# Transposes of the probabilities one step further behind the scores, in two of three attention stages of a fused layer kernel

## What is computed

```python
# mixing: heads A (8, window 128, with sinks), heads B (8: compressed, selected and windowed branches, gated and added)
x = x + 0.5 * swiglu(rms_norm(x, ffn1_norm), ffn1_w_in, ffn1_w_out)
o_a = banded_attention(q_a, k_a, v_a, tbl[:, :8], 128, sinks_a)
o_b = gates[0] * o_cmp + gates[1] * o_sel + gates[2] * o_win
x = x + concatenate([o_a, o_b]) @ w_mix_out
x = x + 0.5 * swiglu(rms_norm(x, ffn2_norm), ffn2_w_in, ffn2_w_out)
# second block, layer 0: chunked attention with a bias by distance; layer 1: attention over latent keys and values
s = q @ k.T * scale + bias
p = softmax(where(valid, s, NEG_INF))
h = h + g1 * ((p @ v) @ wo)
h = h + g2 * conv_ffn(...)
```

## Time and profile before

| | |
|---|---|
| median of 3 runs | 2225.38 us (2224.84 to 2227.58) |
| span of the profiled execution | 2227.7 us |
| TensorE matmul / weight load busy | 98% / 82% |
| VectorE, ScalarE, GpSimd busy | 57%, 40%, 12% |
| mean granted TensorE clock | 0.996 of full |
| mixing with the start of its output matmul | about 483 to 622 us of the span |
| chunked with the start of its output matmul | about 1150 to 1230 us of the span |

### The profile page before, as it was taken

The page is one execution under the profiler, slowest core; times in us unless marked ns, Lnnn a source line. Parts: engine busy times, 40 slices in busy tenths (PEclk is TensorE's granted clock), DMA queues, the critical chain, the costliest instruction groups (busy, mean ns, idle before and its releaser), DMA issues.

```text
span 2227.7 us, 30871 instructions
## 1 busy us (share of the span) xinstructions
PE 2183.2 (98%) x11681; PEld 1820.5 (82%) x11681; DVE 1276.1 (57%) x2136; ACT 899.4 (40%) x1492; POOL 267.9 (12%) x445
## 2 busy tenths in 40 slices
PE   8999999998999999999999999999999999999998
PEld 6888888877888888888888888888878888888887
DVE  5764763557843363365347766465476766545654
ACT  4222223456742222225237544234364755332343
POOL 2110220035400020010017000000000430000000
PEclk9999999999999999999999999999999999999999
DMA  8964993231033274264331333332313212323332
GB/s 265 287 202 131 312 303 104 94 88 39 30 114 106 76 256 149 83 228 159 95 96 49 90 101 88 104 94 85 114 50 97 65 48 76 100 89 104 94 92 97
DMA packets 260212, 270.42 MB, mean 121 GB/s; under 512 B 9190, under 2 KB 202365, under 8 KB 260109
## 3 DMA queue, kind: packets, MB, share of 16 engines
q1 hardware_dynamic: 238381, 190.40, 28.8%
q0 software_dynamic: 21728, 78.63, 10.3%
HBM read 265.72 MB, written 12.72 MB: 125 GB/s over the span
## 4 chain that ended last, share of the span: by engine, by line
PE 84%; DVE 6%; ACT 5%; DMA 3%; issue 2%; POOL 1%; SPq 0%; DVEq 0%; POOLq 0%; ACTq 0%
PE bank L345 15%; PE bank L346 15%; PE bank L347 15%; PE bank L351 11%; PE bank L353 11%; PE bank L352 11%; PE bank L1855 2%; PE bank L1830 2%; PE bank L1808 2%; DMA raw<-in_ffn_w_in_dram 1%; DVE w_lo L328 1%; POOL probs L2026 1%; ACT w_hi L324 1%; ACT probs L1902 1%; ACT xT_hi L773 1%
## 5 line engine op out<-in xcount | busy, mean ns | idle before, releaser
L345 PE MATMUL bank<-xT_hi,w_hi 128*128 128x512 f32 (+1 forms) x1624 | 620.7, 382 | 7.2 <-DVE w_lo L328 3.8
L346 PE MATMUL bank<-xT_lo,w_hi 128*128 128x512 f32 (+1 forms) x1624 | 618.3, 381 | 0.0
L347 PE MATMUL bank<-xT_hi,w_lo 128*128 128x512 f32 (+1 forms) x1624 | 618.3, 381 | 0.0
L328 DVE TENSOR_TENSOR w_lo<-raw,w_hi 128x2048 fp32r<-128x2048 f32 (+2 forms) x200 | 410.9, 2055 | 319.7 <-ACT w_hi L324 317.9
L324 ACT ACTIVATE w_hi<-raw 128x2048 fp32r<-128x2048 f32 (+3 forms) x201 | 345.9, 1721 | 456.2 <-PE bank L353 398.2
L345 PEld LDWEIGHTS bank<-xT_hi,w_hi 128*128 128x128 f32 x1624 | 304.5, 188 | 69.8 <-DVE w_lo L328 4.2
L347 PEld LDWEIGHTS bank<-xT_hi,w_lo 128*128 128x128 f32 x1624 | 304.6, 188 | 59.4
L346 PEld LDWEIGHTS bank<-xT_lo,w_hi 128*128 128x128 f32 x1624 | 304.6, 188 | 58.1
L351 PE MATMUL bank<-w_hi,hid_hi 128*128 128x512 f32 x704 | 274.1, 389 | 0.0
L353 PE MATMUL bank<-w_hi,hid_lo 128*128 128x512 f32 x704 | 273.9, 389 | 0.0
L352 PE MATMUL bank<-w_lo,hid_hi 128*128 128x512 f32 x704 | 273.9, 389 | 0.0
(11 more groups left out here) (330 smaller groups left out, 2766.8 us busy)
## 6 DMA issues: line engine op xcount, KB each, us to landing
raw<-in_ffn_w_in_dram SPq DMA_DIRECT2D x40, 1024.0 KB, 6.1
raw<-in_f_win_dram SPq DMA_DIRECT2D x40, 1024.0 KB, 6.0
mod_w<-in_mod_w_dram POOLq DMA_DIRECT2D x48, 512.0 KB, 5.5
mod_w_more<-in_mod_w_dram POOLq DMA_DIRECT2D x48, 512.0 KB, 5.9
raw<-in_ffn_w_out_dram SPq DMA_DIRECT2D x24, 768.0 KB, 4.6
raw<-in_f_wout_dram SPq DMA_DIRECT2D x24, 768.0 KB, 4.4
raw<-in_a_wqkv_dram SPq DMA_DIRECT2D x12, 1024.0 KB, 5.2
skewed_strips<-bias_strips POOLq DMA_DIRECT2D x32, 320.0 KB, 7.0
```

Of the source, the lines that this page charges most:

```text
L328: dve.tensor_tensor(out=w_lo[:, slot, :n], in0=raw[:, slot, :n], in1=w_hi[:, slot, :n].bitcast(f32), op=ALU.subtract).then_inc(lo_done, 1)
L345: pe.matmul(o, lhsT=w[0], rhs=xs[0], start=first, stop=False)
L346: pe.matmul(o, lhsT=w[0], rhs=xs[1], start=False, stop=False)
L347: return pe.matmul(o, lhsT=w[1], rhs=xs[0], start=False, stop=last)
```

## The change

`PairAttention` gets a `lag` and a rule for the places in `probs`. With lag 1, which latent attention keeps, the order is as before. With lag 2, for mixing and chunked, TensorE does in iteration k scores of k, values of k-3 and transposes of k-2; copies are those of k-2, and the split of bank 7 moves back by one iteration too. There are three places for probabilities and for inverse sums, which move from `stat` to `small`. Mixing has a rule of its own for the places, so that its early steps stay clear of `cmp_w1`. One iteration more is needed to drain, and a third piece of the output matmul is laid into it, so that one piece instead of two stands behind the last values.

```diff
-        probs_0 = take("probs_0", [P, 6, SEQ], at=xT_at)
+        probs_0 = take("probs_0", [P, 9, SEQ], at=xT_at)
...
-        probs_1 = take("probs_1", [P, 6, SEQ], at=xT_at)
+        probs_1 = take("probs_1", [P, 9, SEQ], at=xT_at)
...
             def inverses(self, k, i, m=1):
-                at = 8 + 4 * (k % 2) + i
-                return stat[:, at:at + m]
+                at = 24 + 4 * (k % (self.lag + 1)) + i
+                return small[:, at:at + m]
...
-                for k in range(len(self.steps) + 2):
+                lag = self.lag
+                for k in range(len(self.steps) + lag + 1):
                     if k in beside:
                         beside[k](pe)
                     if k < len(self.steps):
                         self.scores_pe(pe, k)
                     if k in behind:
                         behind[k](pe)
-                    if k >= 2:
-                        self.values_pe(pe, k - 2)
-                    if 1 <= k <= len(self.steps):
-                        self.transposes_pe(pe, k - 1)
+                    if k > lag:
+                        self.values_pe(pe, k - lag - 1)
+                    if lag <= k < len(self.steps) + lag:
+                        self.transposes_pe(pe, k - lag)
...
+                    out_of, copied = k - lag - 1, k - lag
...
-                    if 1 <= k <= len(self.steps):
-                        self.copies(act, k - 1, "act", (0,))
+                    if 0 <= copied < len(self.steps):
+                        self.copies(act, copied, "act", (0,))
...
-                        if k >= 2:
-                            dve.wait_ge(self.t, self.after("t", k - 2))
+                        if k > lag:
+                            dve.wait_ge(self.t, self.after("t", k - lag - 1))
...
+        def probs_0_at(k):
+
+            if k < BANDED - 1:
+                return ((0, 1), (3, 4), (2, 5))[k % 3]
+            return ((6, 7, 8), (3, 4, 5), (0, 1, 2))[(k - BANDED + 1) % 3]
...
-                              probs_0, q0_hi, q0_lo)
+                              probs_0, q0_hi, q0_lo, 2, probs_0_at)
...
-        att_chunked = PairAttention(chunked, probs_1, q1_hi, q1_lo)
+        att_chunked = PairAttention(chunked, probs_1, q1_hi, q1_lo, 2)
...
             def beside(self):
                 k = len(self.att.steps)
-                return {k: lambda pe: self.gemm.piece(pe, 0, 0, [0]), k + 1: lambda pe: self.gemm.piece(pe, 0, 0, [1])}
+                return {k + n: lambda pe, n=n: self.gemm.piece(pe, 0, 0, [n]) for n in range(self.att.lag + 1)}
 
             def pe(self, pe, norm):
-                self.gemm.piece(pe, 0, 0, [2, 3])
+                self.gemm.piece(pe, 0, 0, range(self.att.lag + 1, TOK))
                 self.gemm.piece(pe, 0, 1, range(TOK))
```

More of the change, by code:

```diff
@@ L1717, in program, with __init__ @@
         class PairAttention:
-            def __init__(self, groups, probs, hi, lo):
+            def __init__(self, groups, probs, hi, lo, lag=1, places=None):
                 self.groups, self.probs, self.hi, self.lo = groups, probs, hi, lo
+                self.lag = lag
+                self.places = places or (lambda k: range(3 * (k % (lag + 1)), 3 * (k % (lag + 1)) + 3))
                 self.steps = [step for group in groups for step in group["steps"]]
@@ L1757, in prob @@
             def prob(self, k, unit):
-                at = 3 * (k % 2) + unit.bank
-                return self.probs[:, at, unit.col:unit.col + unit.n]
+                return self.probs[:, self.places(k)[unit.bank], unit.col:unit.col + unit.n]
             def least(self, k, i, m=1):
@@ L1888, in out_act @@
             def out_act(self, act, k):
-                act.wait_ge(self.o, self.after("o", k - 2))
-                act.activation(self.hi[:, self.last[k - 2], :], bank[7][:, :], ACT.Copy).then_inc(self.h, 1)
+                act.wait_ge(self.o, self.after("o", k))
+                act.activation(self.hi[:, self.last[k], :], bank[7][:, :], ACT.Copy).then_inc(self.h, 1)
             def out_dve(self, dve, k):
-                g = self.last[k - 2]
+                g = self.last[k]
                 dve.wait_ge(self.h, self.g0 + g + 1)
@@ L1935, in dve @@
                         behind[k](dve)
-                    early = k - 2 in self.last and self.steps[k - 2].windows is not None
+                    early = out_of in self.last and self.steps[out_of].windows is not None
                     if early:
-                        self.out_dve(dve, k)
+                        self.out_dve(dve, out_of)
                     large = step and step.windows is None and step.sink is None
@@ L1942, in dve @@
                         dve.reciprocal(self.inverses(k, 0, 2), self.sums(k, 0, 2)).then_inc(self.r, 1)
[L1943 to L1946, removed]
+                    if 0 <= copied < len(self.steps):
+                        self.copies(dve, copied, "dve")
+                    if out_of in self.last and not early:
+                        self.out_dve(dve, out_of)
                     if large:
```

16 lines of the change are left out of this document (9 added, 7 removed).

## The result

The changed kernel takes 2231.42 us (median of 21 runs, 2228.31 to 2234.57), the kernel before, run beside it, 2226.69 (21 runs). The ratio is 1.0018, with a 95% interval from 1.0013 to 1.0024: slower by 2.9 to 5.3 us (the medians differ by 4.7), where I had forecast faster by 1.1. The profiled execution of after has a span of 2230.3 us.

What follows compares the result with a forecast made beforehand. No engine was taken as full; waits closing each stage's loop, notably scaled probabilities to transposes, bound it. Mixing -4.1, chunked +1.3 and clock +1.7 gave -1.1 us: 2225.38 to 2224.3 us, 8-in-10 range 2218.5 to 2230.5.

Steps and rivals of the forecast that it cites:

- Mixing, banded steps: Early mixing: small matmuls of step 4 end 6.4 us earlier, the bias of step 8 starts 8.2 us earlier.
- four steps give 1.9 us: Banded steps up to step 8: each costs VectorE some 4.1 us instead of 4.7 to 5.3.
- Mixed groups: Later mixing: groups of 18.79 us shorten by 0.3 to 0.5 each, to VectorE's limit of 18.25 to 18.5.
- Ends: End of mixing and of chunked: 2.5 us of backlog plus a new 2.2 us wait for the weights' split, each.
- nothing upstream lets the split start sooner: Stage end: ScalarE's L1890 of the last group precedes the weights' split and waits for last values; wait of 2.2 us.
- Chunked: Chunked stage: last scores 3.4 us earlier, then 2.5 of backlog and 2.2 of wait, together +1.3 us.
- every other order keeps its distance: Both stages: the change cuts only the link from scaled probabilities to transposes; no size given.
- the period falls to 7.35: Chunked: a group takes 7.35 us instead of 7.64 (bounds 7.25 and 7.64), from three engines' loads.
- Clock: Behind the two new waits of 2.2 us: one fall to half clock of two, +1.7 us (bounds 0 and 3.4).
- The rule of the Trainium skill: GpSimd and VectorE: by their shared SBUF interfaces, more overlap would lengthen GpSimd's rows, 2.7 to 3.1 us in chunked.
- rival 3: Later groups: chunked stays at 7.64 because GpSimd's rows grow, mixed groups gain nothing; +2.1, 2227.5 us; chance 0.15.
- Rival 2: Clock falls more, at both new waits, chunked's start and banded steps, three falls beyond forecast; +5.1, 2230.5 us; chance 0.10.

Runs made afterwards that it cites:

- e10: The kernel after with the two steps of each banded group in mixing in the other order; 2234.38 us (5 runs), 1.0034 of the kernel before.
- e6: The kernel after with the weights split ahead of the last split of bank 7, in mixing and chunked; 2225.44 us, 0.9992 of the kernel before.
- e3: The kernel after with the two steps of each chunked group in the other order, narrow before wide; 2229.99 us, 1.0015 of the kernel before.
- e11: e3 with VectorE's scaled unit of each chunked step cut to 32 columns, so output isn't the reference's; 2228.49 us, 1.0007 of the kernel before.
- e12: The kernel before with VectorE's scaled unit of each chunked step cut to 32 columns, so output isn't the reference's; 2227.63 us, 1.0003 of the kernel before.
- e5: The kernel after with two output matmul pieces beside the attention and two behind the last values, in mixing and chunked; 2225.70 us, 0.9993 of the kernel before.
- e4: The kernel before, lag one, with the two steps of each chunked group in the other order; 2228.70 us, 1.0009 of the kernel before.
- e1: The kernel after with chunked attention back at lag one, so the change in mixing alone; 2224.12 us, 0.9987 of the kernel before.
- e7: The kernel before with a third output matmul piece ahead of the last values in all three attention stages; 2236.96 us, 1.0043 of the kernel before.

## Why the prediction was wrong

1. *Mixing, banded steps.* Right in its mechanism up to step 4. The small matmuls ended 6.2 us earlier against 6.4, waits for scaled units went from 6.1 us to none. The 1.9 us more up to step 8 didn't come: from the end of the small matmuls to step 8 it is 18.2 us before and 18.3 after, so step 8 began 6.1 us earlier, not 8.2. The step that failed is the price of a banded step, "four steps give 1.9 us". Before, 2.8 us of waits for scaled units and 0.7 for q_lo stood in that stretch; after, 0.3 and 2.0 for q_lo, 1.1 for the compression's `cmp_hid_v` and two for biases, 1.0 together. Whether q_lo holds the stretch or VectorE's other work does stays open (e10). Both stretches of half clock of the later banded steps came again, where I kept one; only the early one, of 6.8 us, was gone.
2. *Mixed groups.* 18.79 to 18.29 to 18.38 us, as forecast (18.25 to 18.5); the first of them is shorter, 17.94.
3. *Ends.* 4.6 and 5.3 against 4.7 each; the waits were 1.91 and 1.97 us against 2.2; chunked has 0.55 us for q_lo behind its last scores besides. Right, but the sentence "nothing upstream lets the split start sooner" was wrong. L1890 stands before it in program order alone, and e6 put the split ahead of it and won the wait back.
4. *Chunked.* The step that made the forecast wrong: "every other order keeps its distance", and "the period falls to 7.35". Two errors of one kind are in it. I compared loads (7.21, 7.25, 7.27) and took the waits of PE for the bound. The chain through exponentials, copy and bias took 7.65 with the longer lag (e3, e11) and 7.65 to 7.68 without it (e12), so cutting the other chain won nothing. And a split moved by one iteration, in groups of two steps, went to the side where VectorE is in that chain: 8.02. The start of the stage won its 1.5 us, the groups lost 1.4: -0.1 instead of -3.4.
5. *Clock.* One fall of the two was taken; in the profiled execution both came. The second is more than the +1.4: to the first scores of latent attention (1739.84 before, 1742.76 after) it is +1.7, and the kernel before had 3.4 us of half clock of its own behind them. One fall of two is what the 9 of 17 waits give, so as a mean the term was right. e5 and e6 win 5 to 6 us where the two waits are 3.9; the rest, about 2 us with an error as large, would be the clock behind them.
6. *The rule of the Trainium skill, and rival 3.* In the steady groups GpSimd's row of 512 columns took 1565 ns before and 1554 after, so it did not grow; it did in e3 (1738) and e4 (1650). VectorE's scaled unit of 512 columns took 672 ns before and in e1, 966 in after, 998 in e4 and 579 in e3, where that of 384 columns went from 408 to 750. The Trainium skill (GPSIMD Engine Reference, Specifications) says that GpSimd's SBUF interfaces are shared with VectorE, with contention when VectorE's instruction is in a two-port mode or reads two SBUF inputs. Rows of both engines that change with the schedule would fit that, but GpSimd's row of 512 columns ran beside VectorE's in all four kernels, and no run took GpSimd's work away, so this cause isn't shown. Rival 3's period (7.64) was too short as well, and its mechanism wasn't the one; that the link doesn't hold the later groups by itself was right.

Rival 2 gave 2230.5, near the measured time, by luck: not three more falls came, but one more. By the table, the 6.2 us between forecast and profile are 3.3 of chunked that didn't come, 1.5 of clock, 0.9 of mixing and 0.6 at the end of chunked.

Two sums in the prediction are off by a little and change nothing: 6.4 and 1.9 give 8.3 and not 8.2, and the mixed groups enter with 1.8 where 1.6 was worked out.

## What to carry to other kernels

Before cutting a wait, write down every closed chain through the program order of all engines with its length, not the load of each engine: two chains of nearly the same length hide each other, and the experiment for it is to cut each alone and both together. When an order moves by one iteration in a loop whose iterations alternate, check for each operation of it which kind of iteration it falls into. At the end of such a pipeline look what stands ahead of the next stage's preparation by program order alone: moving that in e6 was worth 5 to 6 us against the kernel after, whose shorter cover had made the wait, twice what the change itself wins in mixing. On the kernel before, where two pieces cover the split, it wasn't run.

## What was not expected of the hardware

Waits of PE of 1.91, 1.97 and 1.98 us, each followed by dense matmuls, were followed by half clock at one place and not at another: in e7 once of three times in the same execution, in after twice of two, in all 9 times of 17. The same VectorE instruction of 512 columns took 579 to 998 ns in the same stage with another schedule around it, GpSimd's 1554 to 1738; what decides it stays open.
